# Turning output rows and attention queries with VectorE transposes and GpSimd block copies in a hybrid decoder layer

## The reference

```python
h = rms_norm(x, norm_w)
proj = h @ w_in                      # 2048 x 8204: 4 retention, 6 delta-rule, 6 attention heads
y_ret  = rms_norm(retention(rq, rk, rv)) * silu(rg)
y_gdn  = rms_norm(gated_delta_rule(conv/silu of gqkv, g, beta)) * silu(gz)
mq, mk = rms_norm(mq, q_norm_w), rms_norm(mk, k_norm_w)
y_moba = softmax_attention(mq, mk, mv, ALiBi, causal) * silu(mz)
out = x + concat(y_ret, y_gdn, y_moba) @ w_out
```

## Time and profile before

| | us |
|---|---|
| median of 3 runs (lowest, highest) | 522.1 (521.22, 522.24) |
| the profiled execution: its own time | 521.48 |
| its span in the trace | 519.7 |
| TensorE busy | 513.7 (99%) |
| VectorE busy | 337.0 (65%) |
| ScalarE busy | 277.0 (53%) |
| GpSimd busy | 91.7 (18%) |

### The profile page before, as it was taken

One profiled execution on the slowest core, in us unless ns is written; L12 is line 12 of the kernel. 1 busy time (PEld: TensorE's weight loads), 2 busy tenths in 40 slices (PEclk: granted clock), 3 DMA queues, 4 the chain that ended last, 5 costly groups with the idle time before them and its releaser, 6 DMA issues.

```text
span 519.7 us, 8821 instructions
## 1 busy us (share of the span) xinstructions
PE 513.7 (99%) x3496; PEld 431.3 (83%) x3496; DVE 337.0 (65%) x529; ACT 277.0 (53%) x439; POOL 91.7 (18%) x84
## 2 busy tenths in 40 slices
PE   8999999999999999999999999999999999999996
PEld 6888888888888888888888888888888888888885
DVE  3999999989765876664644554655366455646551
ACT  5777645654356676565535554664556456443340
POOL 4764253316131312110000000100010010000000
PEclk9999999999999999999999999999999999999999
DMA  8999655765744466576676577657765557758711
GB/s 281 311 293 238 165 138 149 193 154 147 197 124 125 124 160 155 131 202 163 162 186 179 131 212 189 171 160 191 188 178 163 164 158 223 220 177 226 247 40 41
DMA packets 146923, 91.68 MB, mean 176 GB/s; under 512 B 7907, under 2 KB 135874, under 8 KB 146882
## 3 DMA queue, kind: packets, MB, share of 16 engines
q1 hardware_dynamic: 143392, 88.94, 63.0%
q10 hardware_dynamic: 3490, 2.18, 1.5%
HBM read 89.00 MB, written 2.10 MB: 175 GB/s over the span
## 4 chain that ended last, share of the span: by engine, by line
PE 97%; DVE 2%; ACT 0%; issue 0%; POOL 0%; DVEq 0%; POOLq 0%
PE pj L1450 20%; PE pj L1449 20%; PE pj L1447 20%; PE pj L1425 13%; PE pj L1426 6%; PE pj L1495 3%; PE pj L1504 1%; PE mx L1593 1%; PE pj L1422 1%; PE mx L1644 1%; DVE w_lo L353 1%; PE mx L1626 1%; PE mx L1474 1%; PE mx L1714 1%; PE pj L1512 1%; PE mx L1702 1%
## 5 line engine op out<-in xcount | busy, mean ns | idle before, releaser
L353 DVE TENSOR_TENSOR w_lo<-w_raw,w_hi 128x1024 fp32r<-128x1024 f32 x160 | 199.8, 1255 | 92.8 <-ACT w_hi L451 92.5
L451 ACT ACTIVATE w_hi<-w_raw 128x1024 fp32r<-128x1024 f32 x159 | 167.7, 1058 | 135.2 <-PE pj L1450 113.6
L1447 PE MATMUL pj<-w_hi,hT 128*128 128x512 f32 x320 | 127.4, 398 | 0.0
L1449 PE MATMUL pj<-w_hi,hT 128*128 128x512 f32 x320 | 125.9, 393 | 0.0
L1450 PE MATMUL pj<-w_lo,hT 128*128 128x512 f32 x320 | 124.9, 390 | 0.0
L1425 PE MATMUL pj<-hT,w_hi 128*128 128x512 f32 x300 | 109.3, 404 | 0.2 <-DVE w_lo L353 0.2
L1426 PE MATMUL pj<-hT,w_lo 128*128 128x256 f32 x300 | 83.9, 280 | 0.0
L1450 PEld LDWEIGHTS pj<-w_lo,hT 128*128 128x128 f32 x320 | 60.1, 188 | 12.4
L1447 PEld LDWEIGHTS pj<-w_hi,hT 128*128 128x128 f32 x320 | 60.1, 188 | 11.8
L1449 PEld LDWEIGHTS pj<-w_hi,hT 128*128 128x128 f32 x320 | 60.2, 188 | 11.3
L1425 PEld LDWEIGHTS pj<-hT,w_hi 128*128 128x128 f32 x300 | 56.3, 188 | 14.3 <-DVE w_lo L353 1.6
(11 more groups left out here) (241 smaller groups left out, 507.2 us busy)
## 6 DMA issues: line engine op xcount, KB each, us to landing
w_raw<-in_w_in_dram SPq DMA_DIRECT2D x256, 256.0 KB, 3.4
w_raw<-in_w_out_dram SPq DMA_DIRECT2D x64, 256.0 KB, 4.0
big<-in_x_dram SPq DMA_DIRECT2D x9, 256.0 KB, 5.5
out_dram<-sq ACTq DMA_DIRECT2D x7, 256.0 KB, 5.7
big<-in_x_dram SPq DMA_DIRECT2D x3, 512.0 KB, 7.2
cst<-table_dram SPq DMA_DIRECT2D x1, 682.0 KB, 9.8
big<-in_x_dram SPq DMA_DIRECT2D x2, 128.0 KB, 2.6
out_dram<-sq ACTq DMA_DIRECT2D x1, 128.0 KB, 2.4
```

Of the source, the lines that this page charges most:

```text
L353: eng.tensor_tensor(w_lo[:, n % NSPLIT, :], w_raw[:, n % NRAW, :], w_hi[:, n % NSPLIT, :].bitcast(F32), ALU.subtract).then_inc(S("lo"), 1)
L451: act.activation(w_hi[:, n % NSPLIT, :], w_raw[:, n % NRAW, :], ACT.Copy).then_inc(S("hi_done"), 1)
L1447: ins = pe.matmul(bank[:, :], src[:, kc, 0, tok], hi[:, k, :], start=first, stop=False)
L1449: pe.matmul(bank[:, :], src[:, kc, 1, tok], hi[:, k, :], start=False, stop=False)
```

## The change

The 32 TensorE transposes of the five retention and attention pairs' outputs (4 each) and of the three attention pairs' q (4 each) are taken out. In their place:

- VectorE turns the tile with one 32x32-block transpose of 128x512 elements (`turn_rows` for the outputs, one in `mix_moba` for q) into `turned`.
- GpSimd copies the sixteen 32-partition bands to where the full transpose has them (`move_blocks`): copy (q, d) moves 32 partitions by 4 blocks of 32 columns. The copies are issued in four rounds of four; each of the last three rounds first waits for the round before it.
- For q the copies go straight into `qT`; they follow the power of the same pair in GpSimd's queue, and the score products wait for all four copies of the last round. ScalarE's copy from PSUM into `qT` is gone.
- For the outputs the copies go to `spread`. ScalarE and VectorE read `spread` instead of `mx[3]`, and do so at unit `out + 20` and `out + 22` instead of `out + 2`.
- `turned` and `spread` lie in `mT`, which the delta-rule pairs no longer need by then.

```diff
--- before.py
+++ after.py
@@ -103,7 +103,7 @@
 TAP_AT = {116: (1, 0), 124: (1, 1), 130: (1, 2), 142: (1, 3), 198: (2, 0), 200: (2, 1), 208: (2, 2), 220: (2, 3),
           222: (3, 0), 236: (3, 1), U_Y[2] + 7: (4, 0), U_Y[2] + 13: (4, 1), U_CHAIN[0] + 2: (5, 0), U_CHAIN[0] + 6: (5, 1)}
 U_RET = {"tr": 6, "gram": 14, "s1": 20, "o": 28, "out": 52}
-U_MOBA = {"qtr": 5, "ktr": 26, "score": 34, "pt": 54, "o": 62, "out": 72}
+U_MOBA = {"ktr": 26, "score": 34, "pt": 54, "o": 62, "out": 72}
 
 
 def constants():
@@ -270,6 +270,10 @@
 
         both = raw[:, :].rearrange("p h s t -> p (h s t)")[:, 0:8 * T].rearrange("p (n s e) -> p n s e", n=4, s=4)
         rows = [both[:, 2 * h:2 * h + 2] for h in range(2)]
+        FIRST_ROWS = GDN // 2
+        turned = mT[:, 0:4, :]
+        spread = mT[:, 4:8, :]
+        k_turned = mT[:, 8:12, :]
         kT = kq[:, 0].rearrange("p c k t -> p (c k t)")
         qT = kq[:, 1].rearrange("p c k t -> p (c k t)")
 
@@ -719,13 +723,13 @@
 
             def split_rows(p, y0, scales):
 
-                act.wait_ge(S("otr"), p + 1)
+                act.wait_ge(S("otr"), FIRST_ROWS + 4 * (p + 1 - FIRST_ROWS))
                 if len(scales) == 1:
-                    act.activation(yT[:, y0:y0 + 2, 0, :], mx[3][:, :].rearrange("p (h t) -> p h t", h=2), ACT.Copy,
+                    act.activation(yT[:, y0:y0 + 2, 0, :], spread.rearrange("p (h c) t -> p h (c t)", h=2), ACT.Copy,
                                    scale=scales[0]).then_inc(S("yt_hi"), 2)
                 else:
                     for h in range(2):
-                        act.activation(yT[:, y0 + h, 0, :], mx[3][:, h * T:(h + 1) * T], ACT.Copy, scale=scales[h]).then_inc(S("yt_hi"), 1)
+                        act.activation(yT[:, y0 + h, 0, :], spread[:, 2 * h:2 * h + 2, :].rearrange("p c t -> p (c t)"), ACT.Copy, scale=scales[h]).then_inc(S("yt_hi"), 1)
 
             def mix_ret(p, j, base):
                 U = {k: base + v for k, v in U_RET.items()}
@@ -745,7 +749,7 @@
                 act.wait_ge(S("o_psum"), p + 1)
                 act.activation(os_[:, :, :, :], mx[2][:, :].rearrange("p (h c e) -> p h c e", h=2, c=C), ACT.Copy).then_inc(S("os"), 1)
                 squares(p)
-                advance(U["out"] + 2)
+                advance(U["out"] + 20)
                 split_rows(p, Y_BLOCK["ret"] + 2 * j, [sm[:, 96 + 2 * j + h:97 + 2 * j + h] for h in range(2)])
 
             def mix_moba(p, j, base):
@@ -756,9 +760,6 @@
                 act.wait_ge(S("ev_done"), TOK_EV + in_rows(p))
                 for h in range(2):
                     act.activation(sq[:, h], rows[h][:, :, 0:2, :], ACT.Square).then_inc(S("m_sq"), 1)
-                advance(U["qtr"] + 2)
-                act.wait_ge(S("m_qtr"), j + 1)
-                act.activation(qT, mx[3][:, :], ACT.Copy).then_inc(S("m_qT"), 1)
                 gate_tanh(p)
                 advance(U["ktr"] + 2)
                 act.wait_ge(S("m_ktr"), j + 1)
@@ -857,6 +858,28 @@
                         add_halves(*finished(v))
                 pos[0] = max(pos[0], u)
 
+            def spread_rows(p):
+                pool.wait_ge(S("y_turned"), p + 1 - FIRST_ROWS)
+                if p > FIRST_ROWS:
+                    pool.wait_ge(S("yt_lo"), p - FIRST_ROWS)
+                move_blocks(spread, turned, "otr")
+
+            moved = [0]
+
+            def move_blocks(dst, src, done):
+
+                for d in range(4):
+                    if d:
+                        pool.wait_ge(S("moved"), moved[0])
+                    for q in range(4):
+                        a, i = q * QUART, (q ^ d) * QUART
+                        ins = pool.tensor_copy(dst[i:i + QUART, :, a:a + QUART], src[a:a + QUART, :, i:i + QUART])
+                        if d < 3:
+                            ins.then_inc(S("moved"), 1)
+                            moved[0] += 1
+                        else:
+                            ins.then_inc(S(done), 1)
+
             def rms_power(p):
                 pool.wait_ge(S("o_ms"), p + 1)
                 power(56, 52, 4).then_inc(S("o_pow"), 1)
@@ -871,6 +894,10 @@
             def mix_moba(p, j, base):
                 pool.wait_ge(S("m_norm"), j + 1)
                 power(64, 80, 8).then_inc(S("m_pow"), 1)
+                pool.wait_ge(S("m_pow"), j + 1)
+                pool.wait_ge(S("m_qtr"), j + 1)
+                pool.wait_ge(S("o_psum"), p)
+                move_blocks(four(qT), turned, "m_qT")
 
             norms(0, 152)
             norms(1, 208)
@@ -885,8 +912,10 @@
                         split_y(p, Y_BLOCK["gdn"] + 2 * p)
                 elif kind == "ret":
                     rms_power(p)
+                    spread_rows(p)
                 else:
                     mix_moba(p, j, 128 * (p + 1))
+                    spread_rows(p)
 
 
         @block.vector
@@ -1238,15 +1267,21 @@
                     if h == 1:
                         ins.then_inc(S("yf_done"), 1)
 
+            def turn_rows(p):
+                dve.wait_ge(S("on"), p + 1)
+                if p > FIRST_ROWS:
+                    dve.wait_ge(S("otr"), FIRST_ROWS + 4 * (p - FIRST_ROWS))
+                dve.transpose(turned.rearrange("p n c -> p (n c)"), on[:, :, :, :].rearrange("p h c e -> p (h c e)")).then_inc(S("y_turned"), 1)
+
             def split_rows(p, y0, scales):
 
                 dve.wait_ge(S("yt_hi"), 2 * (p + 1) - GDN)
                 if len(scales) == 1:
-                    dve.scalar_tensor_tensor(yT[:, y0:y0 + 2, 1, :], mx[3][:, :].rearrange("p (h t) -> p h t", h=2), scales[0],
+                    dve.scalar_tensor_tensor(yT[:, y0:y0 + 2, 1, :], spread.rearrange("p (h c) t -> p h (c t)", h=2), scales[0],
                                              yT[:, y0:y0 + 2, 0, :].bitcast(F32), ALU.mult, ALU.subtract).then_inc(S("yt_lo"), 1)
                 else:
                     for h in range(2):
-                        ins = dve.scalar_tensor_tensor(yT[:, y0 + h, 1, :], mx[3][:, h * T:(h + 1) * T], scales[h],
+                        ins = dve.scalar_tensor_tensor(yT[:, y0 + h, 1, :], spread[:, 2 * h:2 * h + 2, :].rearrange("p c t -> p (c t)"), scales[h],
                                                        yT[:, y0 + h, 0, :].bitcast(F32), ALU.mult, ALU.subtract)
                     ins.then_inc(S("yt_lo"), 1)
 
@@ -1272,7 +1307,8 @@
                 mean_square(p, False)
                 advance(U["o"] + 18)
                 norm_out(p, False)
-                advance(U["out"] + 2)
+                turn_rows(p)
+                advance(U["out"] + 22)
                 split_rows(p, Y_BLOCK["ret"] + 2 * j, [sm[:, 96 + 2 * j + h:97 + 2 * j + h] for h in range(2)])
 
             def mix_moba(p, j, base):
@@ -1281,9 +1317,11 @@
                 advance(base + 2)
                 for h in range(2):
                     dve.wait_ge(S("m_sq"), 2 * j + h + 1)
-                    dve.tensor_reduce(sm[:, 118 + 4 * h:122 + 4 * h], sq[:, h].rearrange("p c k t -> p (c k) t"), AX.X, ALU.add).then_inc(S("m_nrm"), 1)
-                dve.wait_ge(S("m_nrm"), 2 * j + 2)
+                    dve.tensor_reduce(sm[:, 118 + 4 * h:122 + 4 * h], sq[:, h].rearrange("p c k t -> p (c k) t"), AX.X, ALU.add).then_inc(S("m_step"), 1)
+                dve.wait_ge(S("m_step"), 4 * j + 2)
                 dve.tensor_scalar(sm[:, 80:88], sm[:, 118:126], 1.0 / P, EPS, ALU.mult, ALU.add).then_inc(S("m_norm"), 1)
+                dve.wait_ge(S("otr"), FIRST_ROWS + 4 * (p - FIRST_ROWS))
+                dve.transpose(turned, both[:, :, 0, :]).then_inc(S("m_qtr"), 1)
                 gate(p)
                 advance(base + 12)
                 dve.wait_ge(S("m_pow"), j + 1)
@@ -1294,8 +1332,8 @@
                     head = 2 * j + h
                     slope = 2.0 ** (-8.0 * (head + 1) / MOBA)
                     dve.wait_ge(S("m_lg"), 4 * j + 2 * h + 2)
-                    dve.scalar_tensor_tensor(lg[:, h, :], cst[:, K_DIST:K_DIST + 3 * P], slope, lg[:, h, :], ALU.mult, ALU.add).then_inc(S("m_alibi"), 1)
-                    dve.wait_ge(S("m_alibi"), 2 * j + h + 1)
+                    dve.scalar_tensor_tensor(lg[:, h, :], cst[:, K_DIST:K_DIST + 3 * P], slope, lg[:, h, :], ALU.mult, ALU.add).then_inc(S("m_step"), 1)
+                    dve.wait_ge(S("m_step"), 4 * j + h + 3)
                     for c in range(C):
                         a, b = (0, P) if c == 0 else (P, 3 * P)
                         n = 2 * h + c
@@ -1746,26 +1785,20 @@
                 for n in range(4):
                     ins = pe.matmul(mx[2][:, n * P:(n + 1) * P], aT[:, n, :], rows[n // 2][:, n % 2, 2, :], start=True, stop=True)
                 ins.then_inc(S("o_psum"), 1)
-                stream(U["out"])
-                out_transposes(p, mx[3])
 
             def mix_moba(p, j, base):
                 U = {k: base + v for k, v in U_MOBA.items()}
                 pr = th[:, 6 * P:12 * P].rearrange("p (h c) -> p h c", h=2)
                 pt = [kT, qT]
-                stream(U["qtr"])
```

(7 more changed lines are left out.)

## The result

The changed kernel takes 528.55 us (median of 4 runs, 526.52 to 529.85) against 522.17 us for the kernel before on the same chip: a ratio of 1.012, with a 95% interval from 1.008 to 1.016. It is slower by 6.4 us. The profiled execution took 529.34 us, its span is 527.7 us.

The account below looks back on a forecast made before the run. TensorE, busy 99% of the span, was taken as the bound. -3.6 us for transposes and +8.1 for waits on q gave +4.5: 526.0 from 521.48, or 526.6 us as median of the runs; range 518.2 to 532.5.

Parts of the forecast that it names:

- the hidden case: Rival at q's copies: they take few or no turns with VectorE, q is ready before 338.1; 518.5 us, chance 0.29.
- The transposes' price: On TensorE: eight groups of four transposes go, 0.455 us each, a sure gain of 3.6 us.
- The wait for q: Ahead of the score products: TensorE waits 2.7 us in each of three attention pairs, 8.1 us in all.
- The undisturbed move: On GpSimd: q's sixteen copies without contention take 4.2 us, bounds 2.9 to 12.2 us.
- The turns with VectorE: Behind the power: GpSimd's copies alternate with six VectorE operations that read two SBUF tiles, 6.2 us together.
- the strict case: Turns instruction by instruction: all six VectorE operations get in before the sixteen copies are through; q 4.0 us late.
- the round-wise one: A round of four copies keeps VectorE out until it ends, rounds alternating with single operations; q 1.5 us late.
- The rule on the shared ports: A VectorE operation with two SBUF inputs contends with any GpSimd operation reading SBUF; without it, the whole 3.6 us gained.
- The outputs' moves: At `spread`: up to 9 us contended and 3 us late, covered by tiles made ahead (5.9 us); costed at nothing.
- An end of q's lateness near 1.2 us a pair: Rival at the score products: lateness of about 1.2 us eats the gain; 521 to 523 us, chance 0.07.
- The dear copies: Rival on GpSimd: copies across partitions take 0.5 us and more each; 525.7 up to 542.8 us, chance 0.14.
- held up at `spread`: Rival: ScalarE or VectorE stands so long at `spread` that a tile is late; adds up to 15 us, chance 0.03.

Follow-up runs that it names:

- no low parts: Changed kernel, but the low parts of the four weight tiles VectorE prepares while q is moved are zeros written by a fill that reads nothing; 518.35 us, ratio 0.994.
- half on ScalarE: Changed kernel with the last two of q's four rounds of copies on ScalarE, the first two on GpSimd; 517.70 us, ratio 0.992.
- the outputs alone: Changed kernel with q back on TensorE and ScalarE, so only the outputs are turned by VectorE and GpSimd; 520.12 us, ratio 0.997.
- The filler: Changed kernel with 20 idle TensorE transposes of the identity ahead of the wait for q in each attention pair; 526.15 us, ratio 1.009.
- q alone: Changed kernel with the outputs back on TensorE, so only q is turned by VectorE and GpSimd; 530.72 us, ratio 1.018.

## Why the prediction was right

Its direction, its place and most of its size held: 526.6 us forecast, 528.55 measured. The range, 518.2 to 532.5 us, took in a gain and a loss, so that the time lies in it says little; the stops at the scores, their cause and their length say more.

- *What bounds.* TensorE's chain took every wait in full; nothing later absorbed one. With q in time the time fell to 518.35 and 517.70 us, against 518.5 for the hidden case.
- *The transposes' price.* 3.6 us for eight groups. Without waits 3.5 us (no low parts) and 4.1 (half on ScalarE) came in, 1.7 of 2.3 for the outputs alone. The last two lie half a microsecond on either side of their sums, and the traces put that ahead of the change: counted from the large matmul at 162.03 us to the last one, 2.3 us come in for the outputs alone, and 3.7 with half on ScalarE (162.35 and 511.75 there, 162.03 and 515.11 before).
- *The wait for q.* Forecast 2.7 us a pair, measured 2.7, 2.7 and 2.5. The two terms under it were both off, in opposite directions. The undisturbed move was put at 4.2 us and is 16 x 0.345 = 5.5: the assumption that copies of one round overlap, starting 0.22 us apart, was wrong. They don't overlap, and the waits between rounds cost nothing beside that (0.345 within a round and between rounds). The turns with VectorE were put at 6.2 us for the strict case, or some 3.7 for the round-wise one; they cost 3.5. The mechanism was the strict one, one copy for each of VectorE's operations. Its sum was too dear for two reasons. It counted six operations in full, where the gate and half of the first low part lay beside the power and not beside the copies: 5.1 us are left (331.43 to 336.52). And it put all sixteen copies on top, where five of them pass while VectorE works, 5 x 0.345 = 1.7 us. That the middle between the two cases gives the measured 2.7 us is luck: it was worked out from neither mechanism.
- *The rule on the shared ports.* The Trainium skill (SBUF — State Buffer, section "SBUF: two separate sides") says that a GpSimd operation that reads SBUF and a VectorE operation with two SBUF inputs exclude each other. The runs agree, now for copies with one input: 1.17 us beside a low part, 0.29 beside the sums of squares, which read one tile, and 0.29 beside fills. Whichever starts first blocks the other fully, the Trainium skill says there; as a price this is one-sided here: VectorE gave up less than 0.1 us an operation (2.53 for 2.35) while GpSimd gave up 0.9.
- *The outputs' moves.* They took 8.1 to 9.5 us, as feared, and ScalarE did stand up to 2.8 us at `spread`; no tile and no block of the last pair came late. Costing this at nothing was right.
- *What no step foresaw: the half clock.* Sum of the profiled execution: -3.6 for the transposes, +7.9 for the stops, +3.4 for two stretches at 1.2 GHz (1.6 and 1.8, counted to where the steps are 0.23 us again), together 7.7 us. From the large matmul that starts at 162.03 us before and at 162.61 in the changed kernel, to the last one, at 515.11 and 523.41, it is 7.7 us that are lost. The other 0.6 us were lost ahead of that, where the program is the same; one stop of 0.47 us, which the chain puts on issue at 157 us, is most of it. The filler took the half clock away and left a median of 526.15 us, half a microsecond from the forecast.
- *The rivals.* Hidden copies would have needed 2.7 us more than there were. An end of q's lateness near 1.2 us a pair, worth nothing, was met by a run: the scores at unit 38 with VectorE held at 36. The dear copies (0.5 us and more each) are refuted as a cause: 0.476 to 0.507 is the mean that the page shows, but it mixes 0.29 with 1.17. No tile was held up at `spread`; one a pair was when ScalarE took all of q's copies.

## What to carry to other kernels

Work that leaves the engine that sets the pace gives back only what its replacement's latency does not take from the same engine's next wait; write the replacement's end beside the deadline before moving it. A chain of small GpSimd copies runs at the pace of VectorE's two-input operations beside it, so count those operations in the window, including the ones that the schedule moves in when a deadline is moved. Splitting the chain over two engines brought more here than giving it more time.

## What the runs showed of the hardware

- A GpSimd copy of 32 partitions by 128 elements takes 0.29 us, and copies start 0.345 us apart, whether bands change or not. From the best case of some 1.8 cycles an element in the Trainium skill (GPSIMD Engine Reference, section 3.1) an estimate for the 128 elements alone is 0.19 us; the measured distance is 1.8 times that. The same copy on ScalarE takes one every 0.32 us (2.55 us for eight), and next to VectorE's low parts and its scaling of k each takes the same 0.31 us.
- Stops of TensorE of 2.1 us and more were followed by 1.2 GHz in some cases and not in others: in the profiled executions behind four of six stops of 2.5 to 2.7 us (changed kernel, and q alone) and two of three of 2.1 to 2.3 us. Behind the stops of 1.4 us and less of the other profiled executions it did not come. Two equally long stops of one execution differ in this (2.7 us at 338 and at 390 us), so the length alone doesn't decide; what else does was not tried. It costs 1.6 to 1.8 us each time. It is the larger part of the scatter from run to run: the changed kernel's runs lie 3.3 us apart, those with the filler 0.7.
